# Expert layers of a two-layer backbone: both expert tables streamed through TensorE for groups of 256 tokens, in place of rows gathered for each token

## The reference, cut to what matters

```python
def _peer(h, w_q, keys, u_tab, v_tab):      # 16384 experts = 128 * 128
    # per block of tokens tb:
    q = (tb @ w_q).reshape(tokens, 8, 2, 128)
    s = einsum('thpd,hpnd->thpn', q, keys)              # 16 score rows of 128 per token
    top_s, top_i = top_k(s, 16)
    # for each of 8 heads: 16 x 16 sums of the two halves, the best 16 of them,
    # expert number = top_i[first half] * 128 + top_i[second half]
    # gates = softmax over the 16 kept scores
    # out = sum over the 8*16 chosen experts e of gate * gelu(tb . u_tab[e]) * v_tab[e]
```

## Time and profile before

| | |
|---|---|
| median of three runs | 8560.51 us (8554.86 to 8566.1) |
| span of the profiled execution | 8665.3 us |
| PE busy | 4374.4 us, 50% |
| DVE busy | 4862.0 us, 56% |
| POOL busy | 3388.3 us, 39% |
| ACT busy | 1296.2 us, 15% |
| DMA moved | 1756.13 MB, mean 203 GB/s |
| mean granted clock of PE | 0.764 of full |

### The profile page before, as it was taken

How to read it: one execution, slowest core, us unless ns; L and a number is a source line. 1 busy time by engine, 2 the same in 40 slices (tenths; PEclk the granted TensorE clock), 3 DMA queues, 4 the chain that set the end, 5 groups by cost and what they waited for, 6 DMA issues and landing times. The chain is left out here.

```text
span 8665.3 us, 69664 instructions
## 1 busy us (share of the span) xinstructions
PE 4374.4 (50%) x20060; PEld 2786.3 (32%) x20060; DVE 4862.0 (56%) x9184; ACT 1296.2 (15%) x2609; POOL 3388.3 (39%) x2998
## 2 busy tenths in 40 slices
PE   5966148874142516160607596613887406070716
PEld 1434038862120203030303143403887303030303
DVE  1025653323768786868787202565332487868786
ACT  0013223330010101010101001322333001010100
POOL 0000122320366666767676000012232056767676
PEclk8977569987576868695959797756998759595959
DMA  5220431113498988888898522043011378989898
GB/s 186 80 68 30 136 107 28 35 56 145 187 338 330 334 334 331 330 324 336 319 343 322 184 79 70 26 139 108 27 36 50 116 285 325 340 312 349 315 346 301
DMA packets 609990, 1756.13 MB, mean 203 GB/s; under 512 B 138210, under 2 KB 188466, under 8 KB 603570
## 3 DMA queue, kind: packets, MB, share of 16 engines
q0 software_dynamic: 371520, 1352.83, 42.2%
q1 hardware_dynamic: 220324, 366.53, 12.7%
q10 hardware_dynamic: 17984, 35.12, 1.1%
HBM read 1661.89 MB, written 98.14 MB: 203 GB/s over the span
## 5 line engine op out<-in xcount | busy, mean ns | idle before, releaser
L1484 PE MATMUL ro_ps<-pe_ring,ex_diag 128*128 128x512 f32 x2560 | 1289.7, 634 | 2607.7 <-issue 2142.7
L1418 POOL DMA_INDIRECT pe_ring<-in_peer_v,ex_idx x1280 | 1436.7, 1122 | 750.9 <-issue 339.6
L1523 DVE SCALAR_TENSOR_TENSOR ex_z<-pe_ring,pe_tb 128x1024 f32<-128x1024 f32 x1280 | 1568.1, 1225 | 193.9 <-DVE ex_z L1523 73.9
L1484 PEld LDWEIGHTS ro_ps<-pe_ring,ex_diag 128*128 128x128 f32 x2560 | 463.5, 199 | 3356.8 <-issue 3317.5
L1418 POOL DMA_INDIRECT pe_ring<-in_peer_u,ex_idx x1180 | 1277.2, 1082 | 411.4 <-issue 349.7
L1535 DVE SCALAR_TENSOR_TENSOR ex_y<-pe_ring,ex_wts,ex_y 128x1024 f32<-128x1024 f32 x640 | 822.4, 1285 | 522.2 <-DMA pe_ring<-in_peer_v,ex_idx 465.1
L668 POOL MEMSET pp_w<- 128x512 f32 x2 | 1.1, 525 | 1729.3 <-POOLq L129 1729.3
L312 PE MATMUL p_ps<-p_w,uT 128*128 128x466 f32 x1536 | 619.1, 565 | 32.8 <-PEq L129 27.1
L1027 POOL TENSOR_TENSOR ch_m<-ch_at,ch_joins 128x512 f32<-128x512 f32 x288 | 381.3, 1358 | 167.8 <-DVE ch_at L1163 152.9
L1418 POOL DMA_INDIRECT pe_ring<-in_peer_u,pe_slot x120 | 124.1, 1035 | 738.0 <-PEq L127 702.1
L312 PEld LDWEIGHTS p_ps<-p_w,uT 128*128 128x128 f32 x1536 | 296.9, 194 | 354.4 <-issue 354.4
(11 more groups left out here) (356 smaller groups left out, 7242.0 us busy)
## 6 DMA issues: line engine op xcount, KB each, us to landing
ada_w<-in_w_ada SPq DMA_DIRECT2D x24, 2048.0 KB, 9.4
p_w<-in_w_in SPq DMA_DIRECT2D x16, 1864.0 KB, 8.0
ch_nat<-gd_dram SPq DMA_DIRECT2D x52, 448.0 KB, 3.5
p_dram<-p_out ACTq DMA_DIRECT2D x96, 233.0 KB, 2.0
gd_dram<-pp_gout SPq DMA_DIRECT2D x48, 448.0 KB, 5.6
peer_wq<-in_peer_wq SPq DMA_DIRECT2D x10, 2048.0 KB, 11.1
pe_ring<-in_peer_v,ex_idx POOLq DMA_INDIRECT x1280
pe_ring<-in_peer_u,ex_idx POOLq DMA_INDIRECT x1180
```

Of the source, the lines that this page charges most:

```text
L1418: return pool.indirect_dma_start(dst, None, table, bass.IndirectOffsetOnAxis(ap=index, axis=0))
L1484: mm = pe.matmul(ps[:, 6 + c, :], diag[:, m % DIAGS, :], ring[:, k % RING, c * 512:(c + 1) * 512], start=(m == 0), stop=(m == half - 1))
L1523: v.scalar_tensor_tensor(z[:], ring[:, k % RING, :], 1.0, b["tb"][:], ALU.mult, ALU.mult, accum_out=act_raw[:, k:k + 1]).then_inc(q["dots_ ...
```

## The change

`peer_stages`, `experts_stage`, the routing steps and the loads of the query weights ahead go away. `peer_stage` takes their place. It works on groups of 256 tokens (two tiles): three groups in the first layer, two in the second. An expert's number is i * 128 + j in the reference; the host now lays `u` out as 128 blocks (one for each j), transposed, so that one block of 512 KB holds 128 experts for PE, and `v` likewise. All of a group's hidden values form a matrix `W` of 128 partitions (i) x 128 blocks (j) x 256 tokens, 4 bytes each, so 16 MB in SBUF; smaller buffers live inside it while its parts aren't in use. SP issues every block, through a ring of 7 buffers. Per group:

1. Queries: 16 blocks of 8 matmuls of 256 columns, and 2 score matmuls of 128 columns for each block; ACT copies.
2. U: 128 blocks of 8 matmuls of 256 columns: the dot products of all 16384 experts with all 256 tokens. ACT writes Gelu of each pair of blocks into `W`. Meanwhile DVE chooses the experts for both tiles, with the same operations as before, and after pair 54 of 64 PE transposes expert numbers and gates.
3. Gates: for each token a matrix of 128 x 128 that is zero but for its 128 chosen experts, made as one matmul of two one-hot matrices (K is the slot number). DVE writes the one-hots of 8 tokens at a time (`oa`, `ob`, three buffers each), POOL scales `oa` by the gates, PE multiplies, DVE multiplies `W` by four tokens' results from PSUM.
4. V: 128 blocks of 4 matmuls of 512 columns, accumulated in four PSUM banks.
5. Post-norm of both tiles; for all but the last group it runs on DVE beside the next group's queries.

The hardware loop over the layers becomes a Python loop, so that the whole program is written out once for each layer; that is why every buffer gets a layer number (`sbuf`, `psum`). The loops inside the other stages stay. The diff, cut to its core:

```diff
-        with nc.Fori(0, DEPTH) as l:
+        for l in range(DEPTH):
...
-                    load_queries_part(sp, l, t, wq, pair, 0, wq_in)
...
-                    sp.wait_ge(wq_in, 16)
...
-                peer_stages(nc, l, t, s, wq, consts)
+            peer_stage(nc, l, t, s, consts)
...
+    groups = list(range(l * CTX_TILES, TILES, 2))
...
+                def next_block(n, src):
+
+                    if n >= NB:
+                        sp.wait_ge(block_used, n - NB + 1)
+                    sp.dma_start(ring[n % NB][:], src).then_inc(block_in[n % NB], 16)
...
+                    for n in range(PAIRS):
+                        if n >= 4:
+                            pe.wait_ge(u_kept, PAIRS * gi + n - 3)
+                        else:
+                            pe.wait_ge(s_kept, 8 * gi + 8)
+                        for x in range(2):
+                            w = block_of(at_u(gi, 2 * n + x))
+                            for k in range(KT):
+                                mm = pe.matmul(ps[:, 4 + n % 4, x * GT:(x + 1) * GT], w[:, k * P:(k + 1) * P], tbT[:, k, :],
+                                               start=(k == 0), stop=(k == KT - 1))
+                            mm.then_inc(block_used, 1)
+                        if n == PAIRS - 10:
+                            pe.wait_ge(route_ready, gi + 1)
...
+                    for q in range(QUADS):
+                        bt = q // 2
+                        if q % 2 == 0:
+                            pe.wait_ge(oa_scaled, BATCHES * gi + bt + 1)
+                            pe.wait_ge(ob_ready, BATCHES * gi + bt + 1)
+                        if q >= 4:
+                            pe.wait_ge(g_used, QUADS * gi + q - 3)
+                        else:
+                            pe.wait_ge(u_kept, PAIRS * (gi + 1))
+                        for x in range(4):
+                            j = q % 2 * 4 + x
+                            mm = pe.matmul(ps[:, 4 + q % 4, x * P:(x + 1) * P], oa[bt % NH][:, j, :], ob[bt % NH][:, j, :], start=True, stop=True)
+                        mm.then_inc(g_done, 1)
+
+                    pe.wait_ge(g_used, QUADS * (gi + 1))
+                    pe.wait_ge(slots_ready, 2 * gi + 2)
+                    for j in range(I_BLOCKS):
+                        w = block_of(at_v(gi, j))
+                        for u in range(2):
+                            for c in range(2):
+                                mm = pe.matmul(ps[:, 2 * u + c, :], W[:, j, u * P:(u + 1) * P], w[:, c * 512:(c + 1) * 512],
+                                               start=(j == 0), stop=(j == I_BLOCKS - 1))
+                        mm.then_inc(block_used, 1)
+                        if j == I_BLOCKS - 20 and gi + 1 < NG:
+                            turn(gi + 1)
...
+                        act.activation(W[:, pair_start(n):pair_start(n) + 2, :].rearrange("p a b -> p (a b)"), ps[:, 4 + n % 4], ACT.Gelu).then_inc(u_kept, 1)
...
+                    for bt in range(BATCHES):
+                        pool.wait_ge(oa_ready, BATCHES * gi + bt + 1)
+                        pool.tensor_tensor(oa[bt % NH][:], oa[bt % NH][:], slots[:, 2, bt * BATCH:(bt + 1) * BATCH].unsqueeze(2).to_broadcast([P, BATCH, P]),
+                                           ALU.mult).then_inc(oa_scaled, 1)
...
+                def one_hots(gi, bt):
+
+                    span = slice(bt * BATCH, (bt + 1) * BATCH)
+                    if bt >= NH:
+                        v.wait_ge(g_done, QUADS * gi + 2 * (bt - NH + 1))
+                    v.tensor_tensor(oa[bt % NH][:], slots[:, 0, span].unsqueeze(2).to_broadcast([P, BATCH, P]),
+                                    iota[:].unsqueeze(1).to_broadcast([P, BATCH, P]), ALU.is_equal).then_inc(oa_ready, 1)
+                    v.tensor_tensor(ob[bt % NH][:], slots[:, 1, span].unsqueeze(2).to_broadcast([P, BATCH, P]),
+                                    iota[:].unsqueeze(1).to_broadcast([P, BATCH, P]), ALU.is_equal).then_inc(ob_ready, 1)
+
+                def weigh(gi, q):
+
+                    v.wait_ge(g_done, QUADS * gi + q + 1)
+                    w = W[:, :, 4 * q:4 * q + 4]
+                    v.tensor_tensor(w, w, ps[:, 4 + q % 4].rearrange("p (t i) -> p i t", t=4), ALU.mult).then_inc(g_used, 1)
...
+                    for bt in range(NH):
+                        one_hots(gi, bt)
+                    v.wait_ge(u_kept, PAIRS * (gi + 1))
+                    for bt in range(BATCHES):
+                        weigh(gi, 2 * bt)
+                        weigh(gi, 2 * bt + 1)
+                        if bt + NH < BATCHES:
+                            one_hots(gi, bt + NH)
+                    if gi + 1 < NG:
+                        norm(gi + 1)
+                    finish(gi)
```

More of the change, by code:

```diff
@@ L100, in constants @@
     c["k_iota"] = np.broadcast_to(np.arange(TOPK, dtype=np.float32), (P, TOPK)).copy()
+    c["k_lane"] = np.broadcast_to(np.arange(P, dtype=np.float32), (P, P)).copy()
     c["k_zero"] = np.zeros((2, IN_COLS), np.float32)
@@ L140, in _, with sbuf, psum @@
                         sp.sem_clear(s)
+def sbuf(nc, l, name, shape, dt=F32):
+    return nc.sbuf_tensor(f"{name}{l}", shape, dt)
+def psum(nc, l, name, shape):
+    return nc.psum_tensor(f"{name}{l}", shape, F32)
 def chained(eng, sem):
@@ L428, in _, with attend_stage @@
                         act.activation(b[k][:, :, cols], ps[:, bank, 2:4], ACT.Copy).then_inc(copied, 1)
-def attend_stage(nc, s, b, consts, group, first, last, key_tiles, bias_dram):
+def attend_stage(nc, l, s, b, consts, group, first, last, key_tiles, bias_dram):
     diff = group == "A"
@@ L1205, in _, with scan_post_stage @@
                 sp.wait_ge(last_stored, 16 * 12)
-def load_queries_part(sp, l, t, wq, pair, first, sem):
-    k = sp.snap(first + ((pair + 1) % 2) * 2)
-    sp.dma_start(wq[:, bass.ds(k, 2)], t["peer_wq"][l].rearrange("(k p) n -> p k n", p=P)[:, bass.ds(k, 2)]).then_inc(sem, 16)
-def scan_post_stage(nc, l, t, s, wq, consts):
+def scan_post_stage(nc, l, t, s, consts):
     with ExitStack() as es:
-        sb = lambda n, sh: es.enter_context(nc.sbuf_tensor("po_" + n, sh, F32))
+        sb = lambda n, sh: es.enter_context(sbuf(nc, l, "po_" + n, sh))
         lg, lb, gg = sb("lg", [P, GW]), sb("lb", [P, GW]), sb("gg", [P, HD])
@@ L1225, in scan_post_stage @@
             i = pair * 2
-            with stage(nc, "y0_in", "y1_in", "post0_in", "post1_in", "var_ready", "root_ready", "dve_step", "out_ready", "stored",
-                       "wq_in") as \
-                    (block, y0_in, y1_in, post0_in, post1_in, var_ready, root_ready, dve_step, out_ready, stored, wq_in):
+            with stage(nc, "y0_in", "y1_in", "post0_in", "post1_in", "var_ready", "root_ready", "dve_step", "out_ready", "stored") as \
+                    (block, y0_in, y1_in, post0_in, post1_in, var_ready, root_ready, dve_step, out_ready, stored):
                 y_in, post_in = (y0_in, y1_in), (post0_in, post1_in)
@@ L1305, in mix_stage @@
             with stage(nc, "y0_in", "y1_in", "h0_in", "h1_in", "gate_in", "tr_done", "copied", "mm_done", "var_ready", "std_ready", "dve_step",
-                       "z_ready", "stored", "wq_in") as \
-                    (block, y0_in, y1_in, h0_in, h1_in, gate_in, tr_done, copied, mm_done, var_ready, std_ready, dve_step, z_ready, stored, wq_in):
+                       "z_ready", "stored") as \
+                    (block, y0_in, y1_in, h0_in, h1_in, gate_in, tr_done, copied, mm_done, var_ready, std_ready, dve_step, z_ready, stored):
                 y_in, h_in = (y0_in, y1_in), (h0_in, h1_in)
@@ L1316, in _ @@
                     sp.dma_start(gate[:], over_rows(s["mods"][i, 2 * D:3 * D])).then_inc(gate_in, 16)
-                    load_queries_part(sp, l, t, wq, pair, KT // 2, wq_in)
                     for u in range(2):
@@ L1563, in route_pe @@
-def route_pe(pe, n, ps, b, consts, q):
-    if n < 2:
-        pe.wait_ge(q["tb_ready"], 1)
-        for k in range(4):
-            kk = 4 * n + k
-            tr = pe.transpose(ps[:, n, k * P:(k + 1) * P], b["tb"][:, kk * P:(kk + 1) * P], consts["ident"][:])
-        tr.then_inc(q["tr_done"], 1)
-        return
-    part, g = (n - 2) % 2, (n - 2) // 2
-    if part == 0:
-        pe.wait_ge(q["tbT_ready"], 2)
-        if g >= 2:
-            pe.wait_ge(q["q_ready"], g - 1)
-        for x in range(4):
-            hp = 4 * g + x
-            for k in range(KT):
-                mm = pe.matmul(ps[:, 2 + g % 2, x * P:(x + 1) * P], b["wq"][:, k, hp * P:(hp + 1) * P], b["tbT"][:, k, :], start=(k == 0), stop=(k == KT - 1))
-        mm.then_inc(q["q_done"], 1)
-    else:
-        pe.wait_ge(q["q_ready"], g + 1)
-        if g >= 2:
-            pe.wait_ge(q["s_ready"], g - 1)
-        for x in range(4):
-            hp = 4 * g + x
-            mm = pe.matmul(ps[:, 4 + g % 2, x * P:(x + 1) * P], b["qT"][:, g % 2, x, :], b["keys"][:, hp * PK:(hp + 1) * PK], start=True, stop=True)
-        mm.then_inc(q["s_done"], 1)
@@ L1617, in top16 @@
```

(9 more changed lines are left out.)

556 lines of the change are left out of this document (278 added, 278 removed).

## The result

The changed kernel takes 9746.51 us (9742.87 to 9749.73) beside 8562.11 us for the kernel before on the same chip: 1.1388 times the time, with an interval from 1.1372 to 1.1404. It is slower by 14%. I had predicted 9820 us, with a range of 9600 to 10120. The profiled execution spans 9747.9 us, 1.4 us from the median; the profiled execution of before stood 104.8 us above its own.

What follows compares the result with a forecast made beforehand. Gathers, with bytes as floor, bound the old expert parts (4418 us); five groups of 957 us PE plus 147 us gates, with layer starts and ends, make 5607, 1189 more: span 9854, likeliest 9820 us, range 9600 to 10120.

Steps and rivals of the forecast that it cites:

- PE's stream: Queries, scores, U, V, transposes and step-change waits on PE: 957 us a group with no gap.
- The gate step: Between U and V, DVE's one-hots and POOL's scaling exclude each other: 4.88 us a batch, 147 us a group.
- POOL's term: In the gate step, POOL scales 1024 elements a batch in 2.33 us, from 1152 taking 2.60 and 768 taking 1.80.
- the rival without exclusion: Gate step with DVE alone setting 3.89 us a batch, 118 us in all; 9675 us; chance 0.12.
- I cost these at nothing: On SP's queue, the last group's store, awaiting its post-norm, and 1 MB loads in V would add no time.
- The small waits: Where PE changes steps, waiting for last score copies and the last Gelu: 3.5 us a group, from 0 to 6.
- Bytes are the floor: Expert part of the kernel before: 256 gathers of 512 KB, 134 MB a tile, 268 MB for two tiles.
- the 34 us that I took off for the other case: Forecast 9820, below the 9854 span, in case the profile's 104.8 us excess is spread evenly (9735), not in the gathers.
- PE starved: U and V blocks or PE's instructions arrive late: 700 us more, 10520 us; chance 0.08 for more than 10120.
- POOL between the one-hots: Gate step with POOL between `oa` and `ob`: 6.2 us a batch, 40 us more a group, 10020 us; chance 0.15.
- One pass for each matmul: PE's matmuls take one pass where each took two rows: 2370 us less, 7450 us; chance 0.02.

Runs made afterwards that it cites:

- e5: The changed kernel with four of the eight matmuls of each block of U left out, all blocks still loaded: 8635.98 us, 1.009 of before.
- e3: The changed kernel without POOL's scaling of the one-hots by the gates, POOL only passing the semaphore on: 9663.21 us, 1.1196 of before.
- e1: The changed kernel with SP's store of the last group issued behind the twelfth pair of U's blocks: 9684.55 us, 1.1221 of before.
- e2: The changed kernel with the post-norm's two roots behind query blocks 2 and 5 in ACT's program: 9682.19 us, 1.1217 of before.
- e8: The kernel before with each gather bringing half a row (2 KB), the other half of each buffer zero: 8498.38 us, 0.9931 of before.
- e14: The kernel before with whole rows gathered, but DVE's dot products of u rows over half the columns: 8471.32 us, 0.9893 of before.
- e10: The changed kernel with U's and V's operands rounded to fp32r, 4 ring and 3 copy buffers, roots early, scaling on ACT: 7307.14 us, 0.8539 of before.
- e9: The changed kernel, full f32, with store behind the twelfth pair, roots early and scaling on ACT together: 9624.7 us, 1.1242 of before.
- e11: The rounded kernel e10 with 5 ring buffers and 2 for rounded blocks, not 4 and 3: 7043.64 us, 0.8222 of before.
- e12: The rounded kernel e10 with only the first quarter of each block of U and V loaded: 6752.44 us, 0.7886 of before.

## Why the prediction was right, and where it was not

**PE's stream: right to one per cent.** U with its six transposes took 443.7 us against 447.1, V with the sixteen transposes of the next group's tokens 441.3 against 443.7, queries and scores 62.9 against 62.8. This carried the sum and the sign. e5 shows it from the other side. Together U, its transposes and V took 5.8 us less than I had for a group, 29 us for five.

**The gate step: right in form, POOL's term mis-sized.** I had 4.88 us a batch and 147 us; it is 3.97 and 121. The term that failed is "1152 take 2.60 us and 768 take 1.80, so 2.33 us", read off POOL operations with two full inputs; here, with one input broadcast, it is 1.7 us, worked out above. Whether the broadcast is the reason no run shows. That is 0.63 of the 0.91 us a batch; the one-hots follow each other at 1.14 in place of 1.225 us (0.17), and the handing over that I had at 0.1 isn't there. So a batch without POOL, 3.47 us in e3, is also shorter than my 3.89. That is why the measured 121 us lies beside the 118 us of the rival without exclusion although the exclusion is there; the step's time alone could not have told the two apart. 26 us x 5 = 130 us too much.

**"I cost these at nothing": wrong, 61 us.** The store on SP was to be covered because 7 blocks were in flight and the post-norm takes 16 us. The arithmetic left out that the post-norm needs two roots from ACT, and that on ACT these stand behind all query copies. I had looked at the length of the work and at SP's queue, not at the queue of the engine that it asks. e1 and e2 measure the step.

**The sum.** From my span of 9854: gates -130, U, transposes and V -29, waits between groups +61 make 9756. The span was 9747.9. The small waits that I had at 3.5 us a group were about 1 us (from the first query to U 64.0 us in e1, for 62.9 us of work), 12 us less in all. What is left, 4 us, is the starts and ends of the layers and the other stages. The stream terms are read in one group; in the others V takes 439.7 to 441.5 us. So the forecast was too high by 159 us in two terms and too low by 61 in a third. That part of this cancelled is luck.

**The bound now: wrong, without harm to the number.** "Bytes are the floor" does not hold: half the bytes are worth 0.7% (e8), half of DVE's dot products 1.1% (e14). A DMA share of 0.95 in the `u` half sat beside a DVE close to its own limit: 177 us from first to last dot product, where DVE alone needs the 170.8 of e8. So in that one execution, slower than the median, DVE did not set the `u` half; the gathers most likely did. At the usual speed half of their bytes are worth no more than e8 shows. It did no harm because I took the time of the old part as measured, and never from its bound.

**The excess of the profiled execution: its place was right, and the 34 us that I took off for the other case helped by luck.** The traces show where it lies. Outside the expert parts the profiled execution is like those of e8 and e14: the first expert part starts at 2162.7 us (2162.5 and 2164.4 there), and 2075.3 us lie between the two parts (2074.5 and 2077.5). Inside, a tile takes some 416 us (177 and 239 in the two halves) beside 399 in e8 and 397 in e14. By their medians these edits are worth 6 and 9 us a tile, so about 11 us a tile remain, 110 us for ten, and the excess was 104.8. With the gathers it was gone, so the span was the base and 9854 us what my sum said; it was 106 us too high. Why that execution's gathers were slower stays open. A DMA share near 1 isn't enough: e14 has 0.97, and its span is within 2 us of its median. The kernel before took 72 us more on one chip than on another; whether its profile was taken on such a chip can't be told from it.

**The rivals.** PE starved: not at all; at 151 to 164 GB/s, and even at 301 in e5, PE has no gap in U. POOL between the one-hots: no batch shows it. One pass for each matmul: not in the changed kernel, where rows come in pairs; but e10 shows how much hung on it. I had put that case at 7450 us; with rounded operands and all that goes with them it is 7307, and 7044 with a longer ring. That these lie near each other is chance: I had halved PE's time with DMA at 301 GB/s, and what came was PE's rows at well under half and the bytes as the bound.

## What to carry to other kernels

Before the columns of a dense form are compared with the bytes of a sparse one, count the rows of a matmul in the trace and their length: f32 takes two rows, each longer than the one row of rounded operands, and here this decides between 12% slower (e9) and 18% faster (e11). When a queue waits for a result, follow that result through every engine it visits, with what stands ahead of it in each program, and not only its length. And a DMA share of 0.95 names a bound only if no engine beside it is as near its own: try it with fewer bytes.

## What the runs showed of the hardware that I had not expected

- Operands rounded by an engine to `fp32r` make one row of a matmul where f32 makes two: U of a group goes from 2054 rows and 443 us of busy PE to 1030 rows and 145.5 us (e11): a third and not a half. The row itself is shorter: 216 ns from start to start in f32 (442.95 us / 2054), 145.5 us / 1030 = 141 ns rounded, with ends at gaps counted in. Without the gaps, by the median from one row's start to the next one's, it is 216 and 120 ns at 256 columns (e11), 429 and 233 ns at 512 (e12). Two rows against one make 3.6 to 3.7 times the time. The Trainium skill, FP8 and Floating Point Precision, section "TensorE Precision Notes", says that true f32 makes four passes through the array; the trace comes near it, with 3.6 to 3.7 rows' worth.
- A row of POOL can hold its waiting: `oa` scaled stands at 2.81 us for some 1.7 us of work, and costs DVE only 0.5 us a batch (e3). The mean of such a group is not its price.
- DVE weighs `W` from PSUM read 512 bytes apart in 675 ns for 512 elements, no more than the 688 ns of the same size with plain strides. The doubling that I held possible did not come.
- The kernel before differs by 0.8% between chips (8556.92, 8559.56 and 8628.71 us).
